# The start of a two-layer trunk: tokens and eight modulation weights loaded at once, decay factors and first weights ahead of the row scale, the input's shift added in rounding

## What is computed

```python
def rms_norm(x, eps=EPS):
    xf = x.astype(jnp.float32)
    return (xf * lax.rsqrt(jnp.mean(xf * xf, axis=-1, keepdims=True) + eps)).astype(x.dtype)

def modulate(x, shift, scale):
    return rms_norm(x) * (1.0 + scale) + shift

def adaln(cvec, w_mod_l, b_mod_l):
    m = jax.nn.silu(cvec) @ w_mod_l + b_mod_l
    return jnp.split(m[:, None, :], 6, axis=-1)
...
    hid = jnp.sin(freq * (z @ wf1 + bf1))
    hid = jnp.sin(freq * (hid @ wf2 + bf2))
    filt = (hid @ wf3).astype(jnp.float32)
...
    decay = jnp.exp(-t * deltas)
    return filt * jnp.concatenate([decay, decay], axis=-1)
...
        hc = modulate(xc, mc[0], mc[1])
        hs = modulate(xs, ms[0], ms[1])
```

## Time and profile before

| | |
|---|---|
| median of the runs shown | 1951.58 us (1949.18 to 1954.25, 3 runs) |
| profiled execution | 1955.38 us |
| its span, first to last instruction | 1953.6 us |
| TensorE busy | 1771.7 us, 91% |
| VectorE busy | 850.3 us, 44% |
| ScalarE busy | 564.0 us, 29% |
| GpSimd busy | 104.7 us, 5% |
| mean granted TensorE clock | 0.955 |
| first matmul of unit 1 | 117.27 us from the span's start |

### The profile page before, as it was taken

How to read it: one execution, slowest core, us unless ns; L and a number is a source line. 1 busy time by engine, 2 the same in 40 slices (tenths; PEclk the granted TensorE clock), 3 DMA queues, 4 the chain that set the end, 5 groups by cost and what they waited for, 6 DMA issues and landing times.

```text
span 1953.6 us, 28577 instructions
## 1 busy us (share of the span) xinstructions
PE 1771.7 (91%) x11636; PEld 1605.0 (82%) x11636; DVE 850.3 (44%) x1509; ACT 564.0 (29%) x865; POOL 104.7 (5%) x76
## 2 busy tenths in 40 slices
PE   4989986659799999999999998579799999999997
PEld 2378984427799999999999996447699999999997
DVE  4453228355454433433337345624364333443444
ACT  2133144234342211221214332143343211221223
POOL 1010045000000000000000201000000000000003
PEclk9999998759899999999999998789899999999998
DMA  4544413100344425434434211100132214213212
GB/s 140 162 162 151 130 52 109 30 3 1 109 129 130 132 62 151 129 97 118 131 89 141 83 49 49 38 3 1 44 96 78 64 55 119 65 44 99 81 34 79
DMA packets 235894, 167.91 MB, mean 86 GB/s; under 512 B 7387, under 2 KB 231857, under 8 KB 235410
## 3 DMA queue, kind: packets, MB, share of 16 engines
q1 hardware_dynamic: 235794, 166.49, 28.4%
HBM read 160.61 MB, written 5.87 MB: 85 GB/s over the span
## 4 chain that ended last, share of the span: by engine, by line
PE 84%; DVE 8%; ACT 4%; issue 2%; DMA 1%; POOL 1%; SPq 0%; ACTq 0%; DVEq 0%; POOLq 0%
PE ub L883 11%; PE ua L883 11%; PE ua L885 11%; PE ua L884 11%; PE ub L884 11%; PE ub L885 11%; PE pm L846 3%; PE ua L1073 2%; PE ub L1073 2%; PE pt L1096 1%; PE pm L1096 1%; PE ua L807 1%; PE ua L1084 1%; PE pt L855 1%; DVE hbuf L1818 1%
## 5 line engine op out<-in xcount | busy, mean ns | idle before, releaser
L1541 ACT ACTIVATE whi<-raw 128x1024 fp32r<-128x1024 f32 (+2 forms) x110 | 152.7, 1388 | 692.3 <-PE ub L885 340.2
L1831 DVE TENSOR_TENSOR wlo<-raw,whi 128x2048 fp32r<-128x2048 f32 (+2 forms) x127 | 218.6, 1721 | 80.3 <-ACT whi L1377 39.1
L883 PE MATMUL ub<-in_b_high,whi 128*128 128x386 f32 (+1 forms) x720 | 226.6, 315 | 11.3 <-DVE wlo L1831 7.4
L883 PE MATMUL ub<-in_a_high,whi 128*128 128x384 f32 (+1 forms) x720 | 225.5, 313 | 9.0 <-DVE wlo L1831 9.0
L883 PE MATMUL ua<-in_b_high,whi 128*128 128x386 f32 (+1 forms) x720 | 224.9, 312 | 0.0
L885 PE MATMUL ub<-in_b_high,wlo 128*128 128x386 f32 (+1 forms) x720 | 224.5, 312 | 0.0
L884 PE MATMUL ub<-in_b_rest,whi 128*128 128x386 f32 (+1 forms) x720 | 224.1, 311 | 0.0
L885 PE MATMUL ub<-in_a_high,wlo 128*128 128x384 f32 (+1 forms) x720 | 223.9, 311 | 0.0
L884 PE MATMUL ub<-in_a_rest,whi 128*128 128x384 f32 (+1 forms) x720 | 223.8, 311 | 0.0
L885 PE MATMUL ua<-in_b_high,wlo 128*128 128x386 f32 (+1 forms) x720 | 223.5, 310 | 0.0
L884 PE MATMUL ua<-in_b_rest,whi 128*128 128x386 f32 (+1 forms) x720 | 222.9, 310 | 0.0
(11 more groups left out here) (533 smaller groups left out, 2771.5 us busy)
## 6 DMA issues: line engine op xcount, KB each, us to landing
modw<-in_w_mod SPq DMA_DIRECT2D x44, 1024.0 KB, 5.4
raw<-in_w_ffn_in SPq DMA_DIRECT2D x88, 512.0 KB, 5.1
raw<-in_w_ffn_out SPq DMA_DIRECT2D x32, 512.0 KB, 3.9
raw<-in_w_in_even SPq DMA_DIRECT2D x10, 1024.0 KB, 7.9
raw<-in_w_in_odd SPq DMA_DIRECT2D x7, 1024.0 KB, 5.4
raw<-in_w_ffn_out SPq DMA_DIRECT2D x16, 384.0 KB, 3.4
mod_tail<-in_w_mod SPq DMA_DIRECT2D x4, 1024.0 KB, 5.5
raw<-in_w_out_even SPq DMA_DIRECT2D x8, 512.0 KB, 3.8
```

What stands on the lines that cost most here:

```text
L883: pe.matmul(dst, wh, xh, start=first, stop=False)
L1541: act.activation(whi[s][:, 0:width], raw[s][:, 0:width], ACT.Copy).then_inc(w_hi, 1)
L1831: dve.tensor_tensor(wlo[s][:, 0:width], raw[s][:, 0:width], whi[s][:, 0:width].bitcast(F32), ALU.subtract).then_inc(w_lo, 1)
```

## The change

- SP issues the identity and the tokens first. ScalarE's queue issues the vector rows, `b_mod` and the six filter inputs.
- Once the third token tile has landed, SP issues all eight modulation pieces of the first half of layer 0, into eight places (`mod_first`: five in the area that h will take, the two `modw` and `raw[1]`), then the Fourier matrices, `perm`, `wgate` and unit 0's weights.
- The tokens are copied out of PSUM by ScalarE instead of VectorE. The eight modulation pieces are multiplied and turned among the transposes and the first two projections, in the third bank of `ua` and `ub` (`first_mm`, `first_tr`, `first_row`, `first_reduce`); none is left for the later projections and the spectrum. The projections use two whole sets of PSUM banks.
- The sums of squares come after the second projection; TensorE doesn't wait for the row scale there. On ScalarE the first two decay factors and unit 0's rounded weights stand ahead of the row scale.
- GpSimd's multiplication by `rstd` is gone: VectorE makes x * scale * rstd in one operation (`h_scaled`), ScalarE adds the shift while it rounds, and VectorE takes the rest as (h + shift) - rounded.
- Elsewhere several semaphores are merged (`s_const`, `qk_ld`, `l_ld`) and `after` takes the place of `u_add` and `y_st`; the numbering of the later modulation pieces follows (`MOD_HALF`). Some small tensors have other places.

```diff
+        mod_first = [sb(f"mod_first{m}", [P, 2048], at=hh_at + 8192 * m) for m in range(5)] + [
+            modw[0], modw[1], raw[1]]
...
             sp.dma_start(ident[:, :], i_["c_ident"]).then_inc(s_vec, 16)
-            sp.dma_start(brow[0:96, :], i_["b_mod"].rearrange("l (r p) -> (l r) p", p=P)).then_inc(s_vec, 16)
-            f = lambda name: i_[name][0]
...
             for t in range(TT):
                 src = i_["x_sample"][0, t * P:(t + 1) * P] if t < LS // P else i_["x_prompt"][0]
                 sp.dma_start(xin[:, t], src).then_inc(s_x[t], 16)
-            sp.dma_start(dft[:, :, :], i_["c_dft"].rearrange("(t p) f -> p t f", p=P)).then_inc(f_dl, 16)
-            sp.dma_start(dftp[:, :], i_["c_dft_p"]).then_inc(f_dl, 16)
+            sp.wait_ge(s_x[2], 16)
+            for m in range(MOD_FIRST):
+                src = i_["w_mod"][0, :, m * 256:(m + 1) * 256].rearrange("(k p) n -> p k n", p=P)
+                sp.dma_start(mod_first[m][:, :].rearrange("p (k n) -> p k n", k=KD), src).then_inc(m_first[m], 16)
+            sp.dma_start(dft[:, :, :], i_["c_dft"].rearrange("(t p) f -> p t f", p=P)).then_inc(s_const, 16)
+            sp.dma_start(dftp[:, :], i_["c_dft_p"]).then_inc(s_const, 16)
...
-            mod_load(0, 0, 0, False)
-            mod_load(0, 1, 1, False)
-            for m in range(2, MOD_FIRST):
-                mod_load(0, m, m % 2)
...
             for n, (c0, w) in enumerate(EVEN_COLS):
+                if n == 1:
+                    sp.wait_ge(m_mm, MOD_FIRST)
                 w_load(n, n % 2, wcols(i_["w_in_even"][0], c0, w), KD, w, n >= 2)
...
-            pool.wait_ge(rs_ready, 1)
-            for k in range(KD):
-                if k >= 4:
-                    pool.wait_ge(h_lo, k - 3)
-                pool.tensor_tensor(hbuf[:, k % 4], x[:, k], rstd[:, 0], ALU.mult).then_inc(hx, 1)
...
...
+            def first_mm(n):
+                pe.wait_ge(m_first[n], 16)
+                if n == 0:
+                    pe.wait_ge(sc_ready, 1)
+                if n >= 2:
+                    pe.wait_ge(m_red, n - 1)
+                for kk in range(2):
+                    for j in range(4):
+                        k = 2 * j + kk
+                        ins = pe.matmul(sets[n % 2][32 * j:32 * j + 32, 2, 0:256], sc[:, k, :],
+                                        mod_first[n][:, k * 256:(k + 1) * 256], start=kk == 0, stop=kk == 1)
+                ins.then_inc(m_mm, 1)
+
+            def first_tr(n):
+                pe.wait_ge(m_row, n + 1)
+                for b in range(2):
+                    ins = pe.transpose(sets[n % 2][:, 2, 256 + b * P:256 + (b + 1) * P], modrow[:, b * P:(b + 1) * P],
+                                       ident[:, :])
+                ins.then_inc(m_t, 1)
+
+            filter_layer(0)
+            for k in range(KD):
+                if k >= 2:
+                    pe.wait_ge(xt_c, k - 1)
+                for t in range(TT):
+                    if k == 0:
+                        pe.wait_ge(s_x[t], 16)
+                    dst = sets[k % 2][:, t // 3, (t % 3) * P:(t % 3 + 1) * P]
+                    ins = pe.transpose(dst, xin[:, t, k * P:(k + 1) * P], ident[:, :])
+                ins.then_inc(xt_t, 1)
+                if k >= 2:
+                    first_mm(k - 2)
+                if k >= 3:
+                    first_tr(k - 3)
+                if k == 4:
+                    filter_layer(1)
             pe.wait_ge(f_sin, 2)
             pe.wait_ge(xt_c, KD)
             for t in range(TT):
-                mod_mm_at(t, t // 2, t % 2, first=t == 0)
                 filter_project(t)
-                mod_tr(t, first=t == 0)
+                if t < 2:
+                    first_mm(6 + t)
+                if t < 3:
+                    first_tr(5 + t)
+                if t == 1:
+                    norm_sum(0)
             pe.wait_ge(f_ok, TT)
...
-            pe.wait_ge(f_dl, 32)
+            pe.wait_ge(s_const, 80)
             for n in range(10):
-                if n < MOD_FIRST - TT:
-                    mod_mm_at(TT + n, (TT + n) // 2, (TT + n) % 2)
                 filter_spectrum(n)
-                if n < MOD_FIRST - TT:
-                    mod_tr(TT + n)
...
+            act.wait_ge(s_zero, 1)
...
+                vec(name, i_[name].rearrange("a (r p) -> (a r) p", p=P), rows)
...
+            f = lambda name: i_[name][0]
+            act.dma_start(wf1[:, :], f("w_filt1")).then_inc(f_ld, 16)
+            act.dma_start(zf[:, :], i_["c_z"]).then_inc(f_ld, 16)
+            act.dma_start(wf2[:, :], f("w_filt2")).then_inc(f_ld, 16)
+            act.dma_start(wf3[:, :], f("w_filt3")).then_inc(f_ld, 16)
+            act.dma_start(delta[:, :], i_["c_delta"].to_broadcast([P, HY])).then_inc(f_ld, 16)
+            act.dma_start(negt[:, :], i_["c_negt"]).then_inc(f_ld, 16)
...
-            filter_sine(0)
             for k in range(KD):
-                if k == KD // 2:
-                    filter_sine(1)
+                if k == 3:
+                    filter_sine(0)
+                act.wait_ge(xt_t, k + 1)
+                act.activation(x[:, k, 0:T1], sets[k % 2][:, 0, 0:T1], ACT.Copy)
+                act.activation(x[:, k, T1:T], sets[k % 2][:, 1, 0:T2], ACT.Copy).then_inc(xt_c, 1)
                 act.wait_ge(xt_c, k + 1)
                 square(0, k)
+            filter_sine(1)
+
+            def filter_decay(t):
+                if t >= 2:
+                    act.wait_ge(f_fr, t - 1)
+                act.activation(fdec[:, t % 2], delta[:, :], ACT.Exp, scale=negt[:, t:t + 1]).then_inc(f_dec, 1)
+            filter_decay(0)
+            filter_decay(1)
             def norm_scale(q):
...
             w_high(0, 0, KD * EVEN_COLS[0][1])
-            norm()
+            norm_scale(0)
+            for t in range(2, TT):
+                filter_decay(t)
+
+            def spectrum_out(n):
+                act.wait_ge(g_mm, n + 1)
+                act.activation(gspec[:, n], banks[n % 6], ACT.Copy).then_inc(g_ev, 1)
+            for n in range(4):
+                spectrum_out(n)
+
+            for k in range(KD):
+                act.wait_ge(hmod, k + 1)
+                for v, (a, b) in enumerate(((0, LS), (LS, T))):
+                    ins = act.activation(hhi[:, k, a:b], hbuf[:, k % 4, a:b], ACT.Identity,
+                                         bias=modcol(0, SHIFT + k, v))
+                ins.then_inc(h_hi, 1)
+                if k < 3:
+                    spectrum_out(4 + 2 * k)
+                    spectrum_out(5 + 2 * k)
...
+            def first_row(n):
+                dve.wait_ge(m_mm, n + 1)
+                if n >= 1:
+                    dve.wait_ge(m_t, n)
+                dve.tensor_copy(modrow[:, :], sets[n % 2][:, 2, 0:256]).then_inc(m_row, 1)
+
+            def first_reduce(n):
+                dve.wait_ge(m_t, n + 1)
+                dve.tensor_reduce(mod[:, 0, 2 * n:2 * n + 2, :], sets[n % 2][:, 2, 256:512]
+                                  .rearrange("p (b j v) -> p b v j", b=2, v=32)[:, :, 0:2, :], AX.X, ALU.add
+                                  ).then_inc(m_red, 1)
+
             filter_argument(0)
             for k in range(KD):
-                if k == KD // 2:
-                    filter_argument(1)
-                dve.wait_ge(xt_t, k + 1)
-                dve.tensor_copy(x[:, k, 0:T1], sets[k % 2][:, 0, 0:T1])
-                dve.tensor_copy(x[:, k, T1:T], sets[k % 2][:, 1, 0:T2]).then_inc(xt_c, 1)
                 if k >= 1:
                     add_square(0, k - 1)
+                if k >= 2:
+                    first_row(k - 2)
+                if k >= 3:
+                    first_reduce(k - 3)
+                if k == 4:
+                    filter_argument(1)
             add_square(0, KD - 1)
...
-            for m in range(MOD_FIRST):
-                mod_row(m)
-                if m < TT:
-                    filter_combine(m)
-                mod_reduce(0, m, m)
...
+            for t in range(TT):
+                if t == 2:
+                    w_rest(0, 0, KD * EVEN_COLS[0][1])
+                if t < 2:
+                    first_row(6 + t)
+                if t < 3:
+                    first_reduce(5 + t)
+                filter_combine(t)
...
-            def norm():
-                for k in range(KD):
-                    t = hbuf[:, k % 4]
-                    dve.wait_ge(hx, k + 1)
-                    for v, (a, b) in enumerate(((0, LS), (LS, T))):
-                        ins = dve.tensor_scalar(t[:, a:b], t[:, a:b], modcol(0, SCALE + k, v), modcol(0, SHIFT + k, v),
-                                                ALU.mult, ALU.add)
-                    ins.then_inc(hmod, 1)
-                    if k >= 1:
-                        h_rest(k - 1)
-                h_rest(KD - 1)
+            def h_scaled(k):
+
+                if k >= 4:
+                    dve.wait_ge(h_lo, k - 3)
+                if k == 0:
+                    dve.wait_ge(rs_ready, 1)
```

(23 more changed lines are left out.)

138 lines of the change are left out of this document (48 added, 90 removed).

## The result

| | before | after |
|---|---|---|
| median, us | 1951.58 (1945.21 to 1954.70, 5 runs) | 1934.52 (1931.89 to 1936.41, 5 runs) |
| ratio | | 0.9915, 95% interval 0.9893 to 0.9938 |
| profiled execution, us | 1955.38, span 1953.6 | 1931.89, span 1930.0 |

The forecast was 1940.4 us, its range 1936.5 to 1948.0: the kernel is faster than the range allowed for, by 2.0 us. The profiled execution of before took longer than each of the five runs in the table, and that of after is the fastest of its five; so the profiles differ by 23.5 us and the medians by 17.1.

What follows compares the result with a forecast made beforehand. TensorE bounds the kernel, dense from unit 1 on, so only unit 1's start counts: 16.5 + 60.0 + 17.5 + 12.0 = 106.0 us instead of 117.27. Taking 11.2 us from the median gives 1940.4 us, range 1936.5 to 1948.0 (own range 1937.5 to 1943.5).

Steps and rivals of the forecast that it cites:

- Stage A: First filter matmul to first spectrum matmuls behind the wait for all filters: 60.0 us instead of 65.1.
- Rival 4: TensorE runs stage A at the upper clock, VectorE bounding it at 42 us: 1922.4 us; chance 0.06.
- The shift behind unit 1: From unit 1's first matmul TensorE is dense, so everything behind it moves earlier by the same 11.3 us.
- t0: Start of the first filter matmul, waiting for negt: 16.5 us, bounds 14.6 and 22.5, for 15.03 before.
- The transposes' copies on ScalarE: Copies of x out of PSUM in stage A: with the square 1.8 us a pass, covered by TensorE's 3.6.
- The second argument's hole: Stage A: TensorE waits about 1.9 us while VectorE makes the second filter argument (5.2 us).
- The weights of unit 0: ScalarE's rounding of them (1.05 us) and decay factors, ahead of the row scale: covered by some 8 us.
- Stage B: The spectrum: 17.5 us for 22.5 before; 0.9 us more if the clock rises late.
- Stage C: End of the spectrum to unit 1's first matmul: 12.0 us instead of 14.6, some 0.5 either way.
- Rival 2: Filling the holes does not shorten stage A, passes waiting back and forth: 5.1 us lost, 1945.5; chance 0.09.
- rival 3: Filter inputs get no turn until tokens and all eight weights are through: t0 33.1, 1957.0 us; chance 0.05.
- Rival 1: Large transfers go ahead of the small inputs: t0 22.5, 6 us of the gain lost, 1946.4; chance 0.16.

Runs made afterwards that it cites:

- the filled holes: Kernel before plus five useless float32 matmuls in stage A's holes, results unread: median 1949.89 us, ratio 0.9990.
- the three fillers between the units: Useless matmuls in TensorE's holes, three between units 0 and 1, added to after with modulation weights held and unit 0's weights early: 1927.84 us, ratio 0.9879.

## Why the prediction was wrong

**The step that failed** is in "Stage A": "The work of TensorE in it at the durations of before ... Together 54.5 us". The counts were right, the durations were not: 1.07 instead of 1.87 for a piece, 1.98 instead of 3.71 for a projection, 0.71 to 0.77 instead of 1.07 for a pass of transposes. TensorE's busy time was 35.7 us. The forecast took the clock's level as a property of these operations, on the ground of "30 dense microseconds of the same operations at the lower clock in before". The second profile of before (level up at 71.7 instead of 85.7) and the filled holes (44) show the ground to be a single draw. TensorE's waits in the stage went the other way, 9.2 us for the 5.5 of the sum. In all eight profiles of kernels with mixed pieces and a late row scale it was up by the third piece at the latest, and afterwards it fell only behind waits: after the 3.96 us for the second argument in each of the six where that wait was bare (and in neither of the two where it was filled), and after 0.90 us ahead of the fifth projection in after (3.34), though not in after's second profile (1.98, same wait). With the row scale's wait put back, it fell there and stage A was 58.5 us. That this is close to the forecast's 60.0 is partly luck: the first pieces ran at the upper level, and the 3.08 us of the wait stand in for it. That TensorE standing still is what costs the level is shown by the wait of 3.96 us, bare and filled; for shorter waits the runs show no rule. What brings the level up and lets it stay isn't settled. It is not the mixing as such: it came at 24 to 26 us with the pieces apart and in one profile of the old order too, and was lost there behind the next long wait.

**Rival 4 is what happened**, with 0.06. Its bound by VectorE, 42 us, came near: of its 37.5 us of work VectorE did 34.4, but it stood still for 10.5, not for some 4. It put unit 1 at 88.0 and the median at 1922.4; unit 1 came 4.8 us later, and 0.9 us was lost behind it. The shift behind unit 1, which the sum took as pure, holds to some 4 us: 1833.8 to 1840.3 in the fourteen profiles. The rest of the distance to 1934.5 is between profiles and medians: the profiled execution of before lay 3.8 us above its median, that of after 2.6 below.

**t0** was sized at 16.5 and measured 17.8 and 18.2. Both bounds held; the value was taken too near the lower one, on the ground that at most two weight pieces would be under way, and these with the tokens cost negt 2.7 us more than in before. The 5.25 us that negt took there were themselves one draw: in the second profile of before it landed in 4.12 and t0 was 13.9. Held back, the weights give 14.1, also below the lower bound of 14.6.

**The transposes' copies on ScalarE** were covered, as said. **The second argument's hole** was 1.9 us in the sum and 3.96 in the trace: the passes ahead of it go at the upper level, so TensorE has fewer microseconds in hand while VectorE's 5.2 stay. **The weights of unit 0** ahead of the row scale were covered in after; landing at 46.7 us they were not, and cost some 2 us of stage A.

**Stage B** was right: 17.4 for 17.5, its first twelve records 7.11 us for 3.71 + 2 x 1.72 = 7.15. In the second profile of after it was 18.4, with the 0.9 us on top that the text had kept open for a later rise. **Stage C**: 12.7 for 12.0. VectorE's pair took 0.93 us where I took 0.61 + 0.21 = 0.82, ScalarE's rounding in two 1.0 for 0.8. Five such pairs and one rounding lie on the way to h 7, and they are the 0.7.

**The forecast's own range** was not worked out soundly: its terms (1.9 us of t0 and 0.5 down, 0.9 and 0.5 up) give 1938.0 to 1941.8, not 1937.5 to 1943.5. The measured 1934.52 lies outside either.

**Rival 2** (filled holes don't shorten the stage) and **rival 3** (inputs starved, slower) did not occur. **Rival 1** did so in part: negt was delayed by 2.7 us against the first profile of before (3.8 against the second), not by 6 and more.

**Where the 17 us come from**, by parts undone one at a time: keeping the pieces apart costs all of it (0.9915 to 1.0013), the row scale first some 10 us, the old path of h 1 to 4, the small inputs on SP some 3 (these two by ratios whose intervals overlap with that of after). They sum to more than the whole: the first two each lose the upper level for most of the stage.

## What to carry to other kernels

A duration of TensorE in a stretch with waits is a duration at a level: see at which one it was taken, and work out the sum at both, with the second engine's busy time as the floor of the faster, and give the faster a real chance where the change takes waits away from TensorE. A wait that is put back or left bare can then cost its own length and what follows at half speed (3 us became 13 of stage A here, and some 10 of the median). A profile of one execution is one draw of the level: where runs spread by more than the gain looked for, read a second one before arguing from it.

## What the runs showed of the chip

- The same program got the upper level at 85.7 us in one execution and at 71.7 in another, with nearly equal waits ahead of it, which is part of the 12 us by which runs of before differ.
- Equal waits had unequal ends: 0.90 us ahead of the fifth projection cost the level in one profile of after (3.34) and not in the other (1.98), and with the small inputs on SP 2.13 us in the same place didn't (1.99).
- Of nine profiles with a wait of 2.02 to 2.04 us between units 0 and 1, the level fell within 2 us behind it in six and not in three: before, after's second profile, and the kernel with the pieces apart.
- The granted clock read 1.00 in before both at 1.2 GHz durations and at 2.4, and in after it read 0.54 between 55 and 66 us, once the level had risen and fallen. Ahead of the first rise the level could be seen in the durations of a form alone.
- Where it fell behind such a wait, the granted clock shows it. The windows from 86 to 93 us, unit 1 starting at 89.37 and 89.36 (us, PE, PEld, DVE, ACT, POOL, clock, DMA, GB/s), without and with the three fillers between the units:

```profile
86.00:93.00 7.00, 4.95 (x23) 4.60 (x22) 4.54 (x3) 3.56 (x4) 0.00 (x0) 0.79 0.71 224
```

```profile
86.00:93.00 7.00, 6.99 (x36) 5.37 (x35) 4.53 (x3) 3.56 (x4) 0.00 (x0) 1.00 0.71 219
```
